# Attention scores from rounded halves in two passes a head, their loads on GpSimd, a shorter dt projection, and reordered stage ends

## The chip, the cores and the metric

The kernel runs on one core of a Trainium2 chip. Its engines are TensorE (PE: matrix products; PEld: its weight loads), VectorE (DVE), ScalarE (ACT), GpSimd (POOL) and SyncE (SP, which issues the transfers here), and 16 DMA engines. The metric is the device time of one execution in microseconds (us); lower is better.

## The reference

One layer of a hybrid encoder over two sequences (256 and 1024 rows, together T = 1280 columns in the kernel, where activations are kept transposed, features on the partitions). All in float32.

```
xn = rms_norm(x, g_mix)
q, k, v, gu, gv, z, xbc, dt_raw, gates = split(xn @ w_in)
# A: attention in a band of 128, 8 heads of 64 on 2 key heads
qn, kn = rms_norm(q, q_g) / 8, rms_norm(k, k_g)
scores = qn @ kn.T + bias            # a block of 128 queries sees 3 blocks of keys
out_A  = softmax_with_sink(scores) @ v
# B: out_B = gelu(gu) * (w_s @ layer_norm(gelu(gv)) + b_s)     per chunk of 128
# C: xbc = silu(conv(xbc)); dt = softplus(dt_raw + dt_bias)    2 directions x 16 heads
#    y = ssd_forward + ssd_backward + d * x                    chunks of 128
#    out_C = rms_norm(y * silu(z))
h = x + (sig(gA)*out_A@P_A + sig(gB)*out_B@P_B + sig(gC)*out_C@P_C) @ w_out
y = h + relu(rms_norm(h) @ w1)**2 @ w2
```

## The kernel before, in words

Every dense product is made of three passes in the rounded format f32r (`three_products`, L144): a weight tile and the activations are each split into a rounded high half and a remainder, and hi x hi, lo x hi and hi x lo are summed in PSUM. The 1280 columns go in three groups of 512, 512 and 256 (`GROUPS`); a tile of 128 output features takes 8 steps of 128 input features, so 24 passes a group. ScalarE makes the high half of a weight tile (L176), VectorE the remainder (L181).

Four stages follow one another, each ended by a barrier of all engines:

- `project` (0 to 418 us): the norm of x, then 26 of the tiles of the input projection; between the first ones, the norms of q and k, `dt_products` (behind tile 7) with `turn_dt`, the convolution.
- `attention_and_gmlp` (419 to 721): ten chunks of 128 queries in steps of some 26 us. The rest of the projection's tiles, the late ones (`LateTiles`), is spread over these steps: TensorE does some passes of a late tile (`late.product`) between two pairs of heads in `scores` and `values`. A late group's accumulator is read out by VectorE or ScalarE (`read_out`, L827 and L835).
- `state_space` (722 to 1159): ten chunks forwards, ten backwards (`LAST` is the last), with late tiles between. `finish_y` completes a chunk's y, `add_squares` and `sum_squares` its norm, `normalise` scales it. At the end y of the other branches is loaded and split ahead of the next stage (`ahead`).
- `merge` (1160 to the end): the up products, the output product and the feed-forward layer.

Each engine runs its instructions in the order in which they are written for it; engines wait for one another with semaphores (`wait_ge`, `then_inc`). All DMAs are issued by SyncE, in the order of its own list, and a wait in it holds up what stands behind.

Three places matter here. In `scores`, queries and keys of one key head lie on 64 partitions and those of the other on the other 64, in plain f32; a pair of heads is one product on each half:

```
for g in range(2):
    rows_of = slice(g * HD, (g + 1) * HD)
    pe.matmul(ps_s[:, g, 0:W], q[rows_of, s, j, :], k[rows_of, s, :],
              start=True, stop=True).then_inc(s_full, 1)
between(2 * j)
between(2 * j + 1)
```

`q` and `k` have two buffers (`s`), so a chunk's load can run two chunks ahead. `dt_products` are 8 x 3 passes a column group with 32 output columns (`dtw_hi`, `dtw_lo`), scaled afterwards by the root of x's norm. In `state_space` the wait for a chunk's loads (`loaded`) covers xbc, the factors and both rows of grown.

Of the kernel before, what the change touches and what calls it, by code (L numbers as in the profile page):

```python
# [62 lines left out]
def shape_constants():  # L63
# [25 lines left out]
    return {"masks": masks.astype(f), "onehot": onehot.astype(f), "edge": edge.astype(f)}  # L89
# [25 lines left out]
def build_layer(nc, a, scratch):  # L115

    with ExitStack() as ctx:
# [3 lines left out]
        with ExitStack() as inner:  # L121
            xn = [inner.enter_context(nc.sbuf_tensor(n, [P, KD, T], F32R)) for n in ("xn_hi", "xn_lo")]
            late = LateTiles(ctx, nc, lasting, ws, scratch, xn)
            ab = Split(lasting, "yab", xn)
            with nc.sbuf_tensor("late_result", [P, 2, T], F32) as late.result:
                with nc.sbuf_tensor("bias_sb", [P, HEADS, 3 * P], F32) as bias, nc.sbuf_tensor("root_sb", [P, T], F32) as root:
                    with stage_semaphores(nc) as sem:
                        project(nc, a, scratch, consts, ws, xn, bias, root, late, sem)
                    with stage_semaphores(nc) as sem:
                        attention_and_gmlp(nc, a, scratch, consts, bias, root, late, sem)  # L130
                with stage_semaphores(nc) as sem:
                    state_space(nc, a, scratch, consts, late, ab, sem)
            with stage_semaphores(nc) as sem:
                merge(nc, a, scratch, consts, ws, xn, ab, sem)
# [98 lines left out]
def project(nc, a, scratch, consts, ws, xn, bias, root, late, sem):  # L233
# [4 lines left out]
    with ExitStack() as ctx:  # L238
# [6 lines left out]
        qk_slot = (0, 1, 7)  # L245
        dtw = sb("dtw", [P, KD, 32])
        dtw_hi = sb("dtw_hi", [P, KD, 32], F32R)
        dtw_lo = sb("dtw_lo", [P, KD, 32], F32R)
# [9 lines left out]
        dt_T = sb("dt_T", [32, T])  # L258
# [25 lines left out]
        qk_ready = sem("qk_ready")  # L284
# [3 lines left out]
        stored = [sem(f"stored{s}") for s in range(3)]  # L288
# [8 lines left out]
        dtw_split = sem("dtw_split")  # L297
# [10 lines left out]
        qk_T, uv_T, xbc_T = (scratch[n] for n in ("qk_T", "uv_T", "xbc_T"))  # L308
        END = ((0, 511), (511, 1023), (1023, T))

        def free_at(slot, f):

            return f * 8 - (16 if slot == 0 else 24)

        with nc.Block() as block:
            @block.sync
            def _(sp):
                sp.dma_start(norm_g[:], a["norm_g"]).then_inc(gain_in, 16)
                ws.load(sp, 0, 0)
                for i, (g, lo, hi) in enumerate(PIECES):  # L320
                    t0, n = GROUPS[g]
                    sp.dma_start(x_T[:, lo:hi, t0:t0 + n], a["x_T"][:, lo:hi, t0:t0 + n]).then_inc(x_in[i], 16)
                    if i == 4:
                        ws.load(sp, 1, 1)
                sp.dma_start(masks[:], a["masks"]).then_inc(masks_in, 16)
# [3 lines left out]
                for dst, name in ((qk_g, "qk_g"), (conv_wb, "conv_wb"), (dtw, "w_dt")):  # L329
# [58 lines left out]
                for s, count in enumerate((2 + (N_EARLY - N_QKV) // 2, 3 + (N_EARLY - N_QKV) // 2, 1)):  # L388
                    sp.wait_ge(stored[s], 16 * count)
                sp.wait_ge(root_stored, 16)  # L390
# [7 lines left out]
            def _(pe):  # L398
                def dense(slot, tile):
# [3 lines left out]
                    for g, (t0, n) in enumerate(GROUPS):  # L403
                        if not (known and tile < 2):
# [41 lines left out]
                def dt_products():  # L446
                    pe.wait_ge(dtw_split, 2)
                    pe.wait_ge(scaled, 5)
                    for t0, n in GROUPS:
                        for k in range(KD):  # L450
                            mm = three_products(pe, aux[0:32, t0:t0 + n], dtw_hi[:, k], dtw_lo[:, k],
                                                xn_hi[:, k, t0:t0 + n], xn_lo[:, k, t0:t0 + n], k == 0, k == KD - 1)
                    mm.then_inc(dt_full, 1)

                def turn_v():
                    pe.wait_ge(dt_copied, 1)
# [5 lines left out]
                def turn_dt():  # L462
                    pe.wait_ge(v_ready, 1)
                    for c in range(NT):
                        mm = pe.transpose(aux[:, c * 32:(c + 1) * 32], dt_T[:, c * P:(c + 1) * P], masks[0:32, IDENT, 0:32])
                    mm.then_inc(dt_turned, 1)

                for f in range(F_XBC):
# [3 lines left out]
                    if f == 7:  # L472
# [18 lines left out]
            def _(act):  # L491
# [18 lines left out]

                def square(f):
# [15 lines left out]
                next_weights(0)  # L527
                norm.squares(act, 1)
# [5 lines left out]
                act.wait_ge(small_in, 16 * 5)  # L534
                act.activation(dtw_hi[:], dtw[:], ACT.Identity).then_inc(dtw_split, 1)
                for f in range(5):
                    square(f)
                    next_weights(f + 2)
                    root_of(f)

                def copy_rows(d):
                    act.wait_ge(rows_full, d + 1)
                    act.wait_ge(v_stored if d else stored[2], 16)
# [43 lines left out]
            def _(dve):  # L587
# [14 lines left out]
                def normalise(f):  # L602
# [3 lines left out]
                                             ALU.mult, ALU.mult).then_inc(qk_ready, 1)  # L606

# [8 lines left out]
                ws.low_half(dve, 1, 1)  # L616
                lower_x(2)
# [15 lines left out]
                dve.wait_ge(dtw_split, 1)  # L633
                dve.tensor_tensor(dtw_lo[:], dtw[:], dtw_hi[:].bitcast(F32), ALU.subtract).then_inc(dtw_split, 1)
# [45 lines left out]
                for f in range(2, F_XBC):  # L680
                    if f < 5:
                        out = x_T[:, qk_slot[f % 3]]
                        if f > 2:
                            dve.wait_ge(stored[f % 3], 16)
                    elif f == 5:
                        out = v_raw
                    else:
                        out = x_T[:, f % 2]
                        dve.wait_ge(stored[f % 2], free_at(f % 2, f))
# [5 lines left out]
                    if f == 7:  # L695
                        dve.wait_ge(dt_full, 1)
                        dve.tensor_tensor(dt_T[:], aux[0:32, 0:T], root[0:32], ALU.mult).then_inc(dt_copied, 1)
# [145 lines left out]
class RelativeBias:  # L843
# [39 lines left out]
    def store_rows(self, sp):  # L883
        sp.wait_ge(self.filled, 1)
        for lo in (0, P + T):
            sp.dma_start(self.scratch["qk_T"][4, :, lo:lo + P], self.zeros[:]).then_inc(self.pads_out, 16)
# [15 lines left out]
    def finish(self, sp):  # L902
        sp.wait_ge(self.shifted_in, 16)
        sp.wait_ge(self.pads_out, 64)


def attention_and_gmlp(nc, a, scratch, consts, bias, x_root, late, sem):
# [9 lines left out]
    with ExitStack() as ctx:  # L917
        def sb(name, shape):
# [1343 lines left out]
```

## Time and profile before

| | us |
|---|---|
| median of 3 runs | 2401.06 (2398.81 to 2401.78) |
| the profiled execution | 2400.81 |
| its span in the trace | 2399.0 |
| TensorE busy | 2335.7 (97%) |
| VectorE busy | 1157.5 (48%) |
| ScalarE busy | 841.8 (35%) |
| GpSimd busy | 0.2 (0%) |

Busy times overlap between engines. A matrix product's shown duration is longer than the distance to the next one, since products are pipelined; what a product costs is therefore read from the starts of successive rows. A plain-f32 product stands as two instructions in the rows. The mean granted clock is 0.991 of full speed.

### The profile page before, as it was taken

Reading aid. Unit: us, or ns where it says so; the run is one execution under the profiler, and the core shown is the slowest. Engines: PE = TensorE matmul, PEld = TensorE weight load, DVE = VectorE, ACT = ScalarE, POOL = GpSimd, SP = SyncE. Lnnn points to the kernel's source line nnn. Section 1 sums busy time; section 2 is a strip of 40 time slices with the busy share of each in tenths; the row PEclk is TensorE's granted clock in tenths of the full one; section 3 lists DMA queues with packets and bytes.
Section 4 is the critical chain, followed back from the end, with each engine's and each line's share of the span. In section 5 each row is a group of like instructions: output and inputs, shape, how many; then the busy total and the mean of one; then the engine's idle time right before and its main releaser. Section 6 shows DMA issues by size and latency. Waiting matters only on the chain.

```text
span 2399.0 us, 33028 instructions
## 1 busy us (share of the span) xinstructions
PE 2335.7 (97%) x12944; PEld 1953.3 (81%) x12944; DVE 1157.5 (48%) x1747; ACT 841.8 (35%) x1473; POOL 0.2 (0%) x4
## 2 busy tenths in 40 slices
PE   8999999899998999999799999999999999999999
PEld 6878888677776888887688888788888888888887
DVE  6223454566645666777677444433333333333333
ACT  7423322366655444666434132402021211112120
POOL 0000000000000000000000000000000000000000
PEclk9999999899999999999899999999999999999999
DMA  4223321333327777887563331111111111111112
GB/s 165 78 71 130 125 87 72 109 105 112 122 88 220 229 232 245 267 257 239 205 211 93 106 113 36 36 36 45 36 35 44 35 35 44 35 35 40 39 35 96
DMA packets 167020, 260.29 MB, mean 108 GB/s; under 512 B 11635, under 2 KB 119027, under 8 KB 164252
## 3 DMA queue, kind: packets, MB, share of 16 engines
q1 hardware_dynamic: 166940, 259.19, 33.3%
q8 instruction: 54, 0.88, 0.1%
q14 instruction: 26, 0.21, 0.0%
HBM read 191.54 MB, written 69.71 MB: 109 GB/s over the span
## 4 chain that ended last, share of the span: by engine, by line
PE 50%; DVE 1%; ACT 0%; DMA 0%; issue 0%; DVEq 0%
PE acc L146 16%; PE acc L147 16%; PE acc L148 16%; DVE xn_lo L1805 1%; DVE xn_lo L1803 0%; DMA merged<-s_y_T 0%; ACT xn_hi L1796 0%; PE acc L2079 0%; DVE gates L1924 0%; DVE h_T L2030 0%; ACT sums L2131 0%; ACT sums L2134 0%; ACT L2134 0%; ACT gates L2004 0%; DVE gates L2174 0%
## 5 line engine op out<-in xcount | busy, mean ns | idle before, releaser
L146 PE MATMUL acc<-xn_hi,w_hi 128*128 128x512 f32 (+1 forms) x1944 | 693.5, 357 | 22.1 <-DVE xn_lo L592 9.6
L147 PE MATMUL acc<-xn_hi,w_lo 128*128 128x512 f32 (+1 forms) x1944 | 690.9, 355 | 0.0
L148 PE MATMUL acc<-xn_lo,w_hi 128*128 128x512 f32 (+1 forms) x1944 | 689.9, 355 | 0.0
L146 PEld LDWEIGHTS acc<-xn_hi,w_hi 128*128 128x128 f32 x1944 | 369.2, 190 | 77.8 <-issue 13.9
L148 PEld LDWEIGHTS acc<-xn_lo,w_hi 128*128 128x128 f32 x1944 | 368.8, 190 | 51.7
L147 PEld LDWEIGHTS acc<-xn_hi,w_lo 128*128 128x128 f32 x1944 | 369.1, 190 | 51.2
L176 ACT ACTIVATE w_hi<-w_raw 128x1024 fp32r<-128x1024 f32 x146 | 153.6, 1052 | 555.9 <-PE acc L148 536.0
L146 PE MATMUL late_acc<-xn_hi,w_hi 128*128 128x512 f32 (+1 forms) x768 | 291.0, 379 | 8.2 <-DVE late_result L835 5.8
L148 PE MATMUL late_acc<-xn_lo,w_hi 128*128 128x512 f32 (+1 forms) x768 | 274.4, 357 | 0.0
L147 PE MATMUL late_acc<-xn_hi,w_lo 128*128 128x512 f32 (+1 forms) x768 | 273.8, 356 | 0.0
L147 PE MATMUL acc<-u_hi,w_lo 128*128 128x512 f32 (+1 forms) x768 | 273.6, 356 | 0.0
L146 PE MATMUL acc<-u_hi,w_hi 128*128 128x512 f32 (+1 forms) x768 | 273.6, 356 | 0.0
L148 PE MATMUL acc<-u_lo,w_hi 128*128 128x512 f32 (+1 forms) x768 | 273.6, 356 | 0.0
L2186 DVE TENSOR_TENSOR h_T<-h_T,acc 128x512 f32<-128x512 f32 (+1 forms) x192 | 114.8, 598 | 264.8 <-PE acc L148 264.8
L181 DVE TENSOR_TENSOR w_lo<-w_raw,w_hi 128x1024 fp32r<-128x1024 f32 x146 | 178.7, 1224 | 119.0 <-ACT w_hi L176 117.9
L146 PEld LDWEIGHTS late_acc<-xn_hi,w_hi 128*128 128x128 f32 x768 | 146.9, 191 | 52.5 <-issue 26.2
L147 PEld LDWEIGHTS late_acc<-xn_hi,w_lo 128*128 128x128 f32 x768 | 147.1, 192 | 21.3 <-issue 2.6
L148 PEld LDWEIGHTS late_acc<-xn_lo,w_hi 128*128 128x128 f32 x768 | 146.6, 191 | 20.9
L2144 ACT ACTIVATE u_hi<-gates 128x512 fp32r<-128x512 f32 (+1 forms) x96 | 53.9, 562 | 311.6 <-DVE gates L2174 311.6
L146 PEld LDWEIGHTS acc<-u_hi,w_hi 128*128 128x128 f32 x768 | 144.1, 188 | 23.5
L148 PEld LDWEIGHTS acc<-u_lo,w_hi 128*128 128x128 f32 x768 | 144.1, 188 | 23.5
L147 PEld LDWEIGHTS acc<-u_hi,w_lo 128*128 128x128 f32 x768 | 144.1, 188 | 23.5
(213 smaller groups left out, 2163.2 us busy)
## 6 DMA issues: line engine op xcount, KB each, us to landing
w_raw<-in_w_tiles SPq DMA_DIRECT2D x146, 512.0 KB, 3.7
s_late_T<-late_result SPq DMA_DIRECT2D x32, 640.0 KB, 6.5
c_w<-s_ac SPq DMA_DIRECT2D x20, 1024.0 KB, 4.7
c_grown<-s_grown SPq DMA_DIRECT2D x40, 256.0 KB, 5.6
gates<-s_late_T SPq DMA_DIRECT2D x16, 512.0 KB, 4.5
c_xbc<-s_xbc_T SPq DMA_DIRECT2D x10, 768.0 KB, 4.8
s_xbc_T<-x_T_sb SPq DMA_DIRECT2D x11, 640.0 KB, 3.0
gates<-s_late_T SPq DMA_DIRECT2D x24, 256.0 KB, 2.7
```

Of the source, the lines that this page charges most:

```text
L146: pe.matmul(out, w_hi, x_hi, start=first, stop=False)
L147: pe.matmul(out, w_lo, x_hi, start=False, stop=False)
L148: return pe.matmul(out, w_hi, x_lo, start=False, stop=last)
L176: act.activation(self.hi[:, s], self.raw[:, s], ACT.Identity).then_inc(self.hi_done, 1)
L181: dve.tensor_tensor(self.lo[:, s], self.raw[:, s], self.hi[:, s].bitcast(F32), ALU.subtract).then_inc(self.split_done, 1)
L1805: dve.scalar_tensor_tensor(low, src, self.gain[:, k:k + 1], high, ALU.mult, ALU.subtract).then_inc(self.low, 1)
L2144: act.activation(self.u_hi[:, i, t0:t0 + n], self.relu[:, u % 2, 0:n], ACT.Square).then_inc(self.high, 1)
L2186: dve.tensor_tensor(hh, hh, self.acc2[:, g, 0:n], ALU.add).then_inc(self.added, 1)
```

## The change

- The scores. After their norm, q and k are rounded by ScalarE (`qk_hi`), and VectorE subtracts (`qk_lo`); both are stored. For the scores a head's q has its high half on partitions 0 to 63 and its remainder on 64 to 127, and k's high half stands twice. A head then is one f32r pass of 128 rows (both halves of q with k's high half) and one of 64 rows (q's high half with k's remainder).
- Their loads. GpSimd issues them, into one buffer instead of two: for chunk c it waits until chunk c-1's scores are done.
- dt. `dt_products` move from behind tile 7 to behind tile 0, use raw x and weights times the norm's gain in plain f32, and put the eight steps of 128 features on four groups of 32 output columns, two steps to each. `turn_dt` sums the four groups while it transposes (`fold`).
- Start of attention: VectorE reads the first late result ahead of its next weight remainder; the passes of late tile 1, group 0 stand between the pairs of the first scores.
- State space: xbc has a semaphore of its own, which TensorE waits for; at the start the sums are loaded ahead of grown. At the end, the `ahead` loads are issued a step earlier, the last late group stands ahead of `sum_squares`, and VectorE's last `normalise` of the chunk before comes behind `finish_y`.
- Some buffers are shared or made per stage.

```diff
                 for f in range(5):
                     ws.load(sp, f % 2, f + 6)
-                    sp.wait_ge(qk_ready, f + 1)
-                    slot = f % 3
-                    sp.dma_start(qk_T[f, :, P:P + T], x_T[:, qk_slot[slot]]).then_inc(stored[slot], 16)
+                    for kind, (half, done) in enumerate(((qk_hi, qk_high), (qk_lo, qk_low))):
+                        sp.wait_ge(done, f + 1)
+                        if f == 4:
+                            sp.dma_start(scratch["k_halves"][kind, :, P:P + T], half[:].bitcast(F32)).then_inc(qk_stored, 16)
+                            continue
+                        for g in range(2):
+                            sp.dma_start(scratch["q_halves"][4 * g + f, kind], half[g * HD:(g + 1) * HD].bitcast(F32)).then_inc(qk_stored, 16)
...
                 def dt_products():
-                    pe.wait_ge(dtw_split, 2)
+
+                    pe.wait_ge(dtw_ready, 1)
+                    for t0, n in GROUPS:
+                        for half in range(2):
+                            for i in range(4):
+                                k = 4 * half + i
+                                mm = pe.matmul(aux[32 * i:32 * i + 32, t0:t0 + n], dtw[:, k], x_T[:, k, t0:t0 + n],
+                                               start=half == 0, stop=half == 1)
+                        mm.then_inc(dt_full, 1)
...
                     for c in range(NT):
-                        mm = pe.transpose(aux[:, c * 32:(c + 1) * 32], dt_T[:, c * P:(c + 1) * P], masks[0:32, IDENT, 0:32])
+                        mm = pe.matmul(aux[:, c * 32:(c + 1) * 32], dt_T[:, c * P:(c + 1) * P], fold[:], start=True, stop=True)
...
                 ws.low_half(dve, 1, 1)
+                dve.wait_ge(dtw_in, 16)
+                dve.tensor_tensor(dtw[:], dtw[:], norm_g[:, 0].unsqueeze(2).to_broadcast([P, KD, 32]), ALU.mult).then_inc(dtw_ready, 1)
                 lower_x(2)
...
-        q = sb("q_sb", [P, 2, 4, P])
-        k = sb("k_sb", [P, 2, W])
+        q = sb("q_halves_sb", [P, HEADS, P], F32R)
+        k_hi = sb("k_hi_twice", [P, 2, W], F32R)
+        k_lo = sb("k_lo_sb", [HD, 2, W], F32R)
...
+            @block.gpsimd
+            def _(pool):
+                def load_qk(s, chunk):
+
+                    t0 = chunk * P
+                    if not first(chunk):
+                        pool.wait_ge(s_full, chunk * 8)
+                    if not first(chunk, 2):
+                        pool.wait_ge(m_ready, chunk - 1)
+                    pool.dma_start(q[:], scratch["q_halves"][:, :, :, bass.ds(t0, P)].rearrange("h i d t -> (i d) h t").bitcast(F32R)).then_inc(qk_in[s], 16)
...
-                    for j in range(HEADS // 2):
-                        if not (first(chunk) and j == 0):
-                            pe.wait_ge(s_read, chunk * 8 + 2 * j)
...
-                        between(2 * j)
-                        between(2 * j + 1)
+                    for i, h in enumerate(ORDER):
+                        if not (first(chunk) and i < 2):
+                            pe.wait_ge(s_read, chunk * 8 + (i - 1))
+                        pe.matmul(ps_s[:, i % 2, 0:W], q[:, h], k_hi[:, h // 4], start=True, stop=False)
+                        pe.matmul(ps_s[:, i % 2, 0:W], q[0:HD, h], k_lo[:, h // 4], start=False, stop=True).then_inc(s_full, 1)
+                        if i % 2:
+                            between(i - 1)
+                            between(i)
...
-                scores(0, 0, 48)
+                scores(0, 0, 80, lambda h: late.product(pe, 1, 1, 0, [h]))
...
-                for g in range(NG):
+                for g in range(1, NG):
                     late.product(pe, 1, 1, g)
...
-                late.low_half(dve, 1, 1)
                 for g in range(2):
                     late.read_out_with(dve, 0, 0, g, x_root)
+                late.low_half(dve, 1, 1)
...
+                    if isinstance(n, int) and n == LAST - 1:
+                        sp.wait_ge(y_full, LAST)
+                        for k in range(KD):
+                            sp.dma_start(ahead[k], scratch["y_T"][k, :, 0:512]).then_inc(ahead_in[k // 4], 16)
...
-                    pe.wait_ge(loaded[s], came)
+                    pe.wait_ge(xbc_in[s], came)
...
                         late.product(pe, s, n + BEFORE, 1)
+                        late.product(pe, s, n + BEFORE, 2)
                         sum_squares(n)
-                        late.product(pe, s, n + BEFORE, 2)
...
-                for k in range(2):
-                    ab.remainder(dve, 0, k, ahead[k])
                 finish_y(1, LAST, 1, 16 * NT // 2)
-                for k in range(2, 4):
+                normalise(0, LAST - 1)
+                for k in range(4):
                     ab.remainder(dve, 0, k, ahead[k])
                 add_squares(LAST)
```

How the rows stand then. First TensorE at the start of attention, from the last pass of late tile 0: before, the eight plain-f32 products of the first scores, then the first product with ln_b's rows and late tile 1.

```order
L148 MATMUL late_acc<-xn_lo,w_hi 128x256
L1033 MATMUL ps_scores<-k_sb,q_sb 128x384 x8
L1105 MATMUL ps_gmlp<-w_sT,ln_b_rows 128x128 x4
L146 MATMUL late_acc<-xn_hi,w_hi 128x512
L147 MATMUL late_acc<-xn_hi,w_lo 128x512
```

And with the change:

```order
L148 MATMUL late_acc<-xn_lo,w_hi 128x256
L1073 MATMUL ps_scores<-k_hi_twice,q_halves_sb 128x384
L1074 MATMUL ps_scores<-k_lo_sb,q_halves_sb 128x384
L1073 MATMUL ps_scores<-k_hi_twice,q_halves_sb 128x384
L1074 MATMUL ps_scores<-k_lo_sb,q_halves_sb 128x384
L146 MATMUL late_acc<-xn_hi,w_hi 128x512
L147 MATMUL late_acc<-xn_hi,w_lo 128x512
L148 MATMUL late_acc<-xn_lo,w_hi 128x512
```

L1073 is a pass of 128 rows, L1074 one of 64; they alternate, and six late passes (L146 to L148, twice) stand behind each pair of heads, in the first chunk too.

Next, VectorE at the end of the state-space stage. The names: c_y is y, c_w, c_x_end and c_kept hold the rows loaded ahead, xn_lo their remainders. Before:

```order
L1691 TENSOR_TENSOR c_y<-s_bank_a,c_grown 128x1024
L1655 TENSOR_TENSOR c_y<-c_y,c_y_root 128x1024
L1803 TENSOR_TENSOR xn_lo<-c_w,xn_hi 128x512 x2
L1628 TENSOR_TENSOR c_y<-c_y,s_bank_b 128x1024
L1632 TENSOR_TENSOR c_y<-c_y,c_other 128x1024
L1635 TENSOR_TENSOR c_y<-c_y,c_z 128x1024
L1803 TENSOR_TENSOR xn_lo<-c_w,xn_hi 128x512 x2
L1648 TENSOR_TENSOR c_y_sq<-c_y_sq 128x2x256
```

With the change:

```order
L1746 TENSOR_TENSOR c_y<-s_bank_a,c_grown 128x1024
L1683 TENSOR_TENSOR c_y<-c_y,s_bank_b 128x1024
L1687 TENSOR_TENSOR c_y<-c_y,c_other 128x1024
L1690 TENSOR_TENSOR c_y<-c_y,c_z 128x1024
L1710 TENSOR_TENSOR c_y<-c_y,c_y_root 128x1024
L1857 TENSOR_TENSOR xn_lo<-c_w,xn_hi 128x512 x4
L1703 TENSOR_TENSOR c_y_sq<-c_y_sq 128x2x256
```

The three steps that finish the last chunk's y (L1683 to L1690) stand directly behind the product with grown; the scaling of the chunk before (L1710, L1655 before) and all four remainders of c_w come behind them.

Last, GpSimd's list in the loop over the chunks; before, it had no row in this stage.

```order
L1052 ISA
L1052 DMA q_halves_sb<-s_q_halves 128x8x128
L1054 DMA k_hi_twice<-s_k_halves 64x2x384 x2
L1054 ISA
L1054 DMA k_lo_sb<-s_k_halves 64x2x384
```

These are the loads of one chunk, behind the wait for the last scores of the chunk before (the row in front of q's load).

## Rows read from the trace of the kernel before

**Rows 1.** The page, part 1: busy us (share), instructions.

```profile
PE 2335.7 (97%) x12944; PEld 1953.3 (81%) x12944; DVE 1157.5 (48%) x1747; ACT 841.8 (35%) x1473; POOL 0.2 (0%) x4
```

**Rows 2.** The waits of TensorE: total us, times, longest.

```profile
PE s_bank_d L1530 <- DVE c_y_sq L1650: 11.5, 1, 11.5
...
PE late_acc L146 <- DVE late_result L835: 5.8, 2, 4.1
PE s_bank_a L1473 <- DMA c_grown<-s_grown: 5.6, 1, 5.6
```

**Rows 3.** Timeline of TensorE, dt: start, us, instruction, [idle before].

```profile
135.64 0.39 PE L146 MATMUL aux<-xn_hi,dtw_hi 128*32 128x512 f32 x1
...
149.30 0.28 PE L148 MATMUL aux<-xn_lo,dtw_hi 128*32 128x256 f32 x1
149.42 0.40 PE L146 MATMUL acc<-xn_hi,w_hi 128*128 128x512 f32 x1
```

**Rows 4.** Timeline of TensorE, a plain-f32 product between passes.

```profile
31.45 0.40 PE L148 MATMUL aux<-xn_lo,w_hi 128*128 128x512 f32 x1
31.68 1.02 PE L219 MATMUL late_acc<-root_sb,masks_sb 128*128 128x512 f32 x2
...
32.77 0.40 PE L147 MATMUL aux<-xn_hi,w_lo 128*128 128x512 f32 x1
```

**Rows 5.** Timeline of TensorE, products with v.

```profile
478.24 0.88 PE L1053 MATMUL ps_out<-probs_T,v_sb 128*64 128x128 f32 x12
479.05 0.39 PE L146 MATMUL late_acc<-xn_hi,w_hi 128*128 128x256 f32 x1
```

**Rows 6.** Timeline of TensorE, the transposes of dt.

```profile
179.31 0.80 PE L465 MATMUL aux<-masks_sb,dt_T 32*128 32x32 f32 x10
```

**Rows 7.** Timeline of VectorE, end of the state-space stage.

```profile
1129.93 1.22 DVE L1691 TENSOR_TENSOR c_y<-s_bank_a,c_grown 128x1024 f32<-128x1024 f32 x1
...
1145.77 1.29 DVE L1803 TENSOR_TENSOR xn_lo<-c_w,xn_hi 128x512 fp32r<-128x512 f32 x2
...
1147.70 0.42 DVE L1650 TENSOR_TENSOR c_y_sq<-c_y_sq 128x256 f32<-128x256 f32 x1
...
1151.67 1.23 DVE L1655 TENSOR_TENSOR c_y<-c_y,c_y_root 128x1024 f32<-128x1024 f32 x1 [1.14 <-ACT c_y_root L1569]
```

**Rows 8.** Timeline of TensorE, two pairs of heads in a steady chunk.

```profile
482.87 0.40 PE L148 MATMUL late_acc<-xn_lo,w_hi 128*128 128x512 f32 x1
483.20 0.92 PE L1033 MATMUL ps_scores<-k_sb,q_sb 64*128 64x384 f32 x4
484.05 0.50 PE L146 MATMUL late_acc<-xn_hi,w_hi 128*128 128x512 f32 x1
...
485.62 0.92 PE L1033 MATMUL ps_scores<-k_sb,q_sb 64*128 64x384 f32 x4
```

**Rows 9.** Timeline of TensorE, start of attention to the third chunk's scores, then of ScalarE.

```profile
427.89 1.16 PE L1033 MATMUL ps_scores<-k_sb,q_sb 64*128 64x384 f32 x4
...
435.01 1.65 PE L1033 MATMUL ps_scores<-k_sb,q_sb 64*128 64x384 f32 x4 [1.11 <-DVE scores_sb L1125]
...
451.34 0.39 PE L146 MATMUL late_acc<-xn_hi,w_hi 128*128 128x256 f32 x1 [1.70 <-DVE late_result L835]
...
454.40 0.92 PE L1033 MATMUL ps_scores<-k_sb,q_sb 64*128 64x384 f32 x4
...
480.76 0.92 PE L1033 MATMUL ps_scores<-k_sb,q_sb 64*128 64x384 f32 x4
...
443.40 0.62 ACT L1226 ACTIVATE scores_sb<-scores_sb,softmax_stat 128x384 f32<-128x384 f32 x1 [21.55 <-DVE softmax_stat L1141]
...
448.31 1.04 ACT L176 ACTIVATE w_hi<-w_raw 128x1024 fp32r<-128x1024 f32 x1
```

**Rows 10.** DMA issues: line, count, KB each, us to landing.

```profile
q_sb<-s_qk_T SPq DMA_DIRECT2D x10, 256.0 KB, 4.6
```

**Rows 11.** Timeline of ScalarE, then of TensorE, start of state space.

```profile
733.55 4.77 ACT L1553 ACTIVATE c_w<-c_w,c_factors 128x128 f32<-128x128 f32 x16
...
747.40 1.97 PE L1517 MATMUL s_bank_b<-c_w,c_x_dt 128*64 128x128 f32 x32 [2.18 <-DVE c_state L1695]
```

**Rows 12.** Timeline of SyncE, end of the state-space stage.

```profile
1154.38 0.40 SPq L1400 DMA_DIRECT2D s_y_T<-c_y  x1
1159.73 0.39 SPq L1854 DMA_DIRECT2D merged<-s_y_T  x1
```

More of the change, by code:

```diff
@@ L283, in project @@
         rooted = sem("qk_rooted")
-        qk_ready = sem("qk_ready")
+        qk_ready, qk_high, qk_low, qk_stored = (sem("qk_" + n) for n in ("ready", "high", "low", "stored"))
         curved = sem("uv_curved")
@@ L287, in project @@
         end_step, end_done = sem("end_step"), sem("end_done")
-        stored = [sem(f"stored{s}") for s in range(3)]
+        stored = [sem(f"stored{s}") for s in range(2)]
         root_stored = sem("root_stored")
@@ L403, in dense @@
                     for g, (t0, n) in enumerate(GROUPS):
+                        if known and tile == 1:
+                            pe.wait_ge(dt_copied, g + 1)
                         if not (known and tile < 2):
@@ L471, in _ @@
                         sum_squares(f - 2)
[L472 removed]
+                    if f == 0:
                         dt_products()
@@ L1001, in step @@
                 def step(s, chunk, loads, gated_tile):
-                    if loads:
-                        load_qk(s, chunk + 2)
                     late.load(sp, s, chunk + 4)
@@ L1021, in _ @@
                     sp.wait_ge(y_stored[s], 16 * NT // 2)
+            @block.gpsimd
[7 more added lines that the diff above has]
+                    pool.dma_start(q[:], scratch["q_halves"][:, :, :, bass.ds(t0, P)].rearrange("h i d t -> (i d) h t").bitcast(F32R)).then_inc(qk_in[s], 16)
+                    for i, to in enumerate((k_hi[0:HD], k_hi[HD:P], k_lo[:])):
+                        pool.dma_start(to, scratch["k_halves"][i // 2, :, bass.ds(t0, W)].rearrange("(g d) t -> d g t", g=2)
+                                       .bitcast(F32R)).then_inc(qk_in[s], 16)
+                    pool.dma_start(edge[:, s], a["edge"][bass.ds(chunk, 1)].rearrange("o p e -> p (o e)")).then_inc(qk_in[s], 16)
+                load_qk(0, 0)
+                load_qk(1, 1)
+                with pool.Fori(1, NT // 2) as pair:
+                    for s in range(2):
+                        load_qk(s, pair * 2 + s)
             @block.tensor
@@ L1321, in state_space @@
         ahead_in = [sem(f"s_ahead_in{i}") for i in range(2)]
+        xbc_in = [sem(f"s_xbc_in{s}") for s in range(2)]
         tok_stored, tok_in = ([sem(f"s_{n}{s}") for s in range(2)] for n in ("tok_stored", "tok_in"))
@@ L1430, in step @@
                     store(s, n, c, d)
+                load_xbc(0, 0, 0)
+                load_factors(0, 0, 0)
+                load_sums(0, 0, 0)
+                load_grown(0, 0, 0)
                 sp.dma_start(d_col[:], a["d_col"]).then_inc(col_in, 16)
-                for i in range(2):
-                    load(i, i, 0)
-                    load_sums(i, i, 0)
+                load(1, 1, 0)
+                load_sums(1, 1, 0)
                 with sp.Fori(0, NT // 2 - 1) as pair:
@@ L1450, in _ @@
                         step(s, n, LAST - n, 1, LAST - 2 - n, 1)
-                step(0, LAST - 1, *chunk_of(LAST - 1), None, None)
-                sp.wait_ge(y_full, LAST)
-                for k in range(KD):
-                    sp.dma_start(ahead[k], scratch["y_T"][k, :, 0:512]).then_inc(ahead_in[k // 4], 16)
-                step(1, LAST, *chunk_of(LAST), None, None)
+                for n in (LAST - 1, LAST):
+                    step(n % 2, n, *chunk_of(n), None, None)
                 late.all_stored(sp, BEFORE + 2 * NT)
@@ L1695, in step @@
                         dve.tensor_tensor(state[:], kept[:], bank_b[:], ALU.add).then_inc(state_ready, 1)
-                    if normal:
+                    if normal and not is_last(n):
                         normalise(1 - s, n - 1)
```

155 lines of the change are left out of this document (81 added, 74 removed).

## The prediction

> **What bounds the kernel now.** The page's first part comes first: TensorE is busy for 2335.7 us of 2399.0 and VectorE for 48% [rows 1]. Time moves only with TensorE's own passes, or with the few places where it stands still. The list of TensorE's waits gives those places [rows 2]: 11.5 us at the end of the state-space stage, 5.8 at the start of attention, 5.6 at the start of the state-space stage. Each part of the change meets either a run of passes or one of these waits. The sum is made against the profiled execution, 2400.8 us (span 2399.0), 0.25 us under the median of 2401.06. About 0.2%, 4.8 us, is what a measurement of this kernel can tell from no change.
>
> **dt projection.** Now 72 passes run from 135.64 to 149.42, 13.8 us [rows 3]. They go, and 24 plain-f32 products come behind tile 0: eight for each of the three column groups of 512, 512 and 256. One such product of 512 columns takes 32.77 - 31.68 less the pass of 0.23 (31.68 - 31.45) that stands in between, 0.86 us [rows 4]. One after another, the 24 would take 8 x 2.5 x 0.86 = 17.2; with the four 32-column groups side by side, 4.3. For side by side speak the products with v, which use two 64-column groups: six products of 128 columns would take 6 x 0.86/4 = 1.28 one after another, and are done in 479.05 - 478.24 = 0.81 [rows 5]. No row has four groups; I take 4.3 and 0.6 for entering and leaving, 4.9. Turning dt is ten 32-row transposes now, 0.8 [rows 6], and becomes ten plain-f32 products with 128 rows of weights; at some 0.1 for each of their two instructions, 2.1: +1.3. VectorE gets a multiplication of 128 x 256 ahead of the last part of x's remainder, for which TensorE waits at that point of the program; a row of that size is 0.42 [rows 7]. Sum: -13.8 + 4.9 + 1.3 + 0.4 = **-7.2**, at worst +5 (serial).
>
> **Halves of q and k.** Five roundings on ScalarE, five subtractions on VectorE, 18 stores in place of 5. A subtraction of 1024 columns is some 1.22 [rows 7], so 1.5 for 1280. They stand once a tile of some 17 us of TensorE's passes, on engines that are idle for half the time [rows 1]: 0. If nothing hid them, VectorE's five would show with +7.5.
>
> **Scores.** Now two heads are two plain-f32 products on the two halves of the rows at once. A pair of heads with its six late passes repeats every 485.62 - 483.20 = 2.42 us [rows 8]. The six passes are 6 x 0.23 = 1.37, so the pair costs 1.05. Its stream alone is 0.86 x 384/512 = 0.64. The other 0.41 is the price of entering and leaving the 64-row layout, 0.2 each; half of the entry can be read directly: the scores start 483.20 - 482.87 = 0.33 behind the last late pass, where late passes start 0.23 apart, and 484.05 - 483.20 = 0.85 is left for the stream and the exit. Plain f32 alone has no such price, since the 0.86 of rows 4 is four bare passes of some 0.215.
>
> The new pair is four f32r passes of 0.23 x 384/512 = 0.17, in the order 128 rows, 64, 128, 64, and then the late passes, which are 128 again. The stream, 0.69, is no shorter than now, and there are four changes of layout where there were two: 0.69 + 0.8 = 1.49, +0.44 a pair. The first pair of a chunk comes from the v products, which have a layout of their own, so it has five changes instead of two: +0.64. A chunk costs 3 x 0.44 + 0.64 = 1.96 more, and nine chunks **+17.6** (the first chunk is in the next term). This is the largest term, and it hangs on the 0.2. Bounds: with no price at all a pair is 0.69 instead of 1.05 and a chunk gains 1.24, -11.2 over nine; with 0.3 for each change it is +33. I take 0.2, since rows 8 have the same 64 rows.
>
> The Trainium skill, "TensorEngine Tiling (Array Packing)", section Tiling Modes, Key Properties, says that a change of the tiling mode, and not of the tile alone, drains TensorE. The 0.41 us around a pair agrees with it. By that rule the new order drains four times a pair, which is the sum above; were a switch free, the stage would gain 11.
>
> **Loads by GpSimd.** q and both halves of k now land in one buffer instead of two, so a chunk's load can be issued only after the last score of the chunk before. A step is 480.76 - 454.40 = 26.4 us [rows 9]; the new scores with the passes between them take 3 x (1.49 + 1.37) + 1.49 = 10.1 of it. That leaves 16.3 us for 512 KB of q and 576 KB of k. SyncE's 256 KB of q land in a median of 4.6 [rows 10]; four times the bytes, if they took four times as long, would be 18. No row shows a load issued by GpSimd. I take 8 to 14, hidden: 0. From 16.3 on, each us shows almost in full, eight times.
>
> **Start of attention.** VectorE reads the first late result before it lowers a weight, which saves about 2 of the 4.1 us that TensorE waits [rows 2]. But the first scores wait for GpSimd's first loads; I take 428, about where they start now (427.89, rows 9). One late group of 5.5 us (24 passes) is moved in between them, away from behind them. From the last score (435.01 + 1.65 = 436.66) to the late group at 451.34 there are 14.7 us of VectorE's bias and maxima, ScalarE's exponents from 443.40 and weight at 448.31, VectorE's weight and read-out [rows 9]. Beside these, TensorE will have some 7 us of work instead of 13. The last score ends at 428 + 3 x 2.86 + 1.5, and 2 more for the half clock that is seen here (1.65 for four instructions that take 0.92 later, rows 8 and 9): 440. With 14.7: 454.8. The late group behind it, 3.06 now (454.40 - 451.34), takes about twice that after 7 us of idling: 461, and the second chunk's scores, still at half clock, lose another 1 to 2. Against 454.40: **+8**, from 0 (early loads, no clock lost) to +14 (loads 5 us late).
>
> **Start of the state-space stage.** TensorE waits 5.6 us for c_grown, the last of its loads [rows 2], and would now wait for xbc alone. But behind it ScalarE's decays run from 733.55, and the products that need them start at 747.40 [rows 11]; they hang on the sums, which move ahead of grown by two issues only. **-1.5**, from 0 to -2.2.
>
> **End of the state-space stage.** The merge's first rows of y are loaded after the last chunk's products instead of after the store of the chunk before, some 13 us earlier. VectorE, which waited for ScalarE's rounding of them, goes straight on at 1129.93 + 1.2 = 1131.1 [rows 7]: three steps of 1.2 that finish y, one of 1.2 that scales the chunk before, four remainders of 0.62 (1.29 for two less overlap), two squares (1.1). The squares end at 1139.6, now at 1148.1. Behind them, the scaled y follows after 4.8 (1151.67 + 1.23 - 1148.1, rows 7), its store at 1154.38, and the merge's first load 5.35 after the store [rows 12]. With the same steps y is ready at 1144.4, and the merge starts at 1149.8 instead of 1159.73: **-10**, from -7 to -11. TensorE's 11.5 us of waiting becomes a wait for the new stage.
>
> **Sum.** 2400.8 - 7.2 + 17.6 + 8 - 1.5 - 10 = 2407.7. The moved buffers cost nothing: no instruction waits for them in place of another.
>
> **The rivals.**
> (a) The 64-row f32r passes pay nothing for a change. For it: the 72 passes of 32 columns, f32r in a narrow layout, pay nothing (24 x (0.23 + 0.23 + 0.12) = 13.9 against 13.8, the 0.12 from 149.42 - 149.30, rows 3). Against it: rows 8, which have the rows halved, not the columns. Then 2400.8 - 7.2 - 11.2 + 6 - 1.5 - 10 = 2377, faster. The change as a whole breaks even at 0.155 a change of layout: 9 x (17 x 0.155 - 1.44) = 10.7, what the other terms give.
> (b) GpSimd's loads land more than 16.3 us after the last score. For it: 1088 KB in short rows, into one buffer. Against it: 4.6 us for a quarter of the bytes, and a queue of their own. With 20 us, 8 x 3.7 = 30, more with a lost clock: 2438 to 2457.
> (c) The four 32-column groups run one after another: +12.9, 2421.
> (d) The stage ends do not give their 11.5 back, since another load of the new stage lands last: 2419.
>
> **Chances.** The forecast as summed 0.58, its own range 2399 to 2417; (a) 0.18; (b) 0.12; (c) 0.06; (d) 0.06. The range reaches down to (a) and up past (c): 2374 to 2424; it leaves out (b). Faster, under 2396, 0.20: (a) and a little of the forecast; same, up to 2405.6, 0.23: its lower part; slower 0.57.
>
> **What would show it.** A pair with its passes every 2.86 us in the steady chunks (2.06 if (a) holds); dt's products done within 5 us behind tile 0 (17 in (c)); no wait for q's load ahead of the scores, or one (b); some 7 us of idling ahead of the second chunk's late group; the merge's first load some 10 us earlier against the stage's start. The prediction is wrong above all if a change between two f32r layouts has another price than between f32r and plain f32.

## The result and the profile after

The changed kernel takes 2413.34 us in the median of five runs (2409.16 to 2414.68), the kernel before 2400.14 in its five: a ratio of 1.005, 95% interval 1.0035 to 1.0065. That is slower by 13 us; the forecast was 2408, with a range of 2374 to 2424. The profiled execution took 2410.82, with a span of 2408.4, 9.4 more than before's.

Where the 9.4 us lie is read from one event at each stage's border, the difference between before and after being taken from one border to the next. All times are starts in us, except that the first row is an end.

| border | before | after | after less before, since the border above |
|---|---|---|---|
| project's last pass done, TensorE idle | 418.36 | 411.21 | -7.15 |
| second chunk's scores | 454.40 | 455.60 | +8.35 |
| last products with v | 714.08 | 733.01 | +17.73 |
| last chunk's y products (state space) | 1129.02 | 1149.50 | +1.55 |
| merge's first load | 1159.73 | 1169.27 | -10.94 |
| end of the span | 2399.0 | 2408.4 | -0.14 |

The list of TensorE's waits of the changed kernel (total us, times, longest one), beside [rows 2]:

```profile
PE acc L146 <- PEq L113: 8.6, 1, 8.6
PE late_acc L146 <- DVE late_result_a L865: 8.3, 2, 6.3
PE ps_scores L1073 <- DMA edge_sb<-in_edge: 6.2, 1, 6.2
PE s_bank_b L1560 <- DVE c_x_end L1729: 6.1, 1, 6.1
```

Before, the list also had:

```profile
PE acc L146 <- PEq L112: 6.5, 1, 6.5
```

The 11.5 us for s_bank_d are gone; the wait at the next stage's start has grown from 6.5 to 8.6 (PEq is TensorE's sequencer behind the barrier). New are 6.2 us for GpSimd's first loads and 6.3 ahead of the second chunk's late group (1.7 there before). The 5.6 for c_grown have become 6.1 for c_x_end. What VectorE's steps around c_x_end wait for stands in its timeline:

```profile
754.25 0.42 DVE L1720 COPY c_b_tok<-s_bank_c 128x256 f32<-128x256 f32 x1 [12.13 <-DMA c_d_col<-in_d_col]
754.59 0.42 DVE L1721 TENSOR_TENSOR c_cb<-s_bank_c,masks_sb 128x256 f32<-128x256 f32 x1
754.92 1.22 DVE L1729 TENSOR_TENSOR c_x_end<-c_x_tok,c_factors 128x1024 f32<-128x1024 f32 x1
...
762.08 1.23 DVE L1741 TENSOR_TENSOR c_w<-c_w,c_cb 128x1024 f32<-128x1024 f32 x1 [3.66 <-ACT c_w L1610]
```

c_d_col is the skip column. The change issues it last of the stage's first loads, where before it came first; the description of the change leaves this out. VectorE's first step waits for it, but a few steps later VectorE waits another 3.66 us for ScalarE's decays, so it is the decays that end last here.

The timeline of TensorE for dt, beside [rows 3] and [rows 6]:

```profile
27.02 4.50 PE L461 MATMUL aux<-x_T_sb,dtw 128*32 128x512 f32 x48
...
31.45 0.50 PE L146 MATMUL aux<-xn_hi,w_hi 128*128 128x512 f32 x1
...
170.79 2.31 PE L477 MATMUL aux<-fold_sb,dt_T 128*128 128x32 f32 x20
```

The 24 products (48 instructions) take 31.45 - 27.02 = 4.43 us; the turning takes 2.31.

The timeline of TensorE in a steady chunk, beside [rows 8]:

```profile
539.69 0.88 PE L1094 MATMUL ps_out<-probs_T,v_sb 128*64 128x128 f32 x12
540.50 0.44 PE L1073 MATMUL ps_scores<-k_hi_twice,q_halves_sb 128*128 128x384 f32 x1
540.87 0.43 PE L1074 MATMUL ps_scores<-k_lo_sb,q_halves_sb 64*128 64x384 f32 x1
541.24 0.44 PE L1073 MATMUL ps_scores<-k_hi_twice,q_halves_sb 128*128 128x384 f32 x1
541.61 0.44 PE L1074 MATMUL ps_scores<-k_lo_sb,q_halves_sb 64*128 64x384 f32 x1
541.98 0.50 PE L146 MATMUL late_acc<-xn_hi,w_hi 128*128 128x512 f32 x1
...
543.47 0.34 PE L1073 MATMUL ps_scores<-k_hi_twice,q_halves_sb 128*128 128x384 f32 x1
543.74 0.44 PE L1074 MATMUL ps_scores<-k_lo_sb,q_halves_sb 64*128 64x384 f32 x1
...
546.36 0.34 PE L1073 MATMUL ps_scores<-k_hi_twice,q_halves_sb 128*128 128x384 f32 x1
```

The starts of the four passes lie 0.37 apart, where a pass of 384 columns streams for 0.17. Entered from the late passes (543.47), the first pass, still in their layout, takes only 0.27 until the 64-row pass starts. A pair with its six late passes repeats every 2.89 us (546.36 - 543.47; 2.87 for later ones), before 2.42. The step from chunk to chunk is 28.33 us (540.50 to 568.83), before 26.35.

DMA issues of GpSimd (count, KB each, median us to landing) and the first two rows of its timeline for one chunk:

```profile
q_halves_sb<-s_q_halves POOLq DMA_DIRECT2D x10, 512.0 KB, 7.3
...
edge_sb<-in_edge POOLq DMA_DIRECT2D x10, 2.0 KB, 9.4
```

```profile
466.46 0.89 POOL L1052 DMA_DIRECT2D q_halves_sb<-s_q_halves  x1 [25.88 <-PE ps_scores L1074]
...
469.10 0.65 POOL L1056 DMA_DIRECT2D edge_sb<-in_edge  x1
```

The last of a chunk's loads lands about 469.1 + 9.4 = 478.5, 12 us after the first issue; the scores that need them start at 483.83.

The timeline of SyncE at the end of the state-space stage, beside [rows 12]:

```profile
1164.49 0.38 SPq L1451 DMA_DIRECT2D s_y_T<-c_y  x1
1169.27 0.40 SPq L1908 DMA_DIRECT2D merged<-s_y_T  x1
```

The last y is stored 1164.49 - 1149.50 = 15.0 us after the last chunk's products, 25.4 before (1154.38 - 1129.02).

### The profile page after: what moved, and what is told of

Read it like the earlier page. It is cut to its first block, busy times and chain, and to the rows that moved or that the text cites. A ratio compares the mean times of both kernels' runs of the same rounds, so it can differ in the third digit from the quotient of the medians.

```text
span 2408.4 us, 33121 instructions
## 1 busy us (share of the span) xinstructions
PE 2347.7 (97%) x12930; PEld 1964.3 (82%) x12930; DVE 1169.6 (49%) x1752; ACT 849.6 (35%) x1480; POOL 33.3 (1%) x54
## 4 chain that ended last, share of the span: by engine, by line
PE 49%; DVE 1%; ACT 0%; DMA 0%; issue 0%; DVEq 0%
PE acc L146 16%; PE acc L147 16%; PE acc L148 16%; DVE xn_lo L1859 1%; DVE xn_lo L1857 0%; DMA merged<-s_y_T 0%; ACT xn_hi L1850 0%; PE acc L2133 0%; DVE gates L1978 0%; DVE h_T L2084 0%; ACT sums L2185 0%; ACT sums L2188 0%; ACT L2188 0%; ACT gates L2058 0%; DVE gates L2228 0%
## 5 line engine op out<-in xcount | busy, mean ns | idle before, releaser
L146 PE MATMUL acc<-xn_hi,w_hi 128*128 128x512 f32 (+1 forms) x1944 | 693.9, 357 | 24.3 <-DVE xn_lo L615 9.6
L148 PE MATMUL acc<-xn_lo,w_hi 128*128 128x512 f32 (+1 forms) x1944 | 690.0, 355 | 0.0
L146 PEld LDWEIGHTS acc<-xn_hi,w_hi 128*128 128x128 f32 x1944 | 369.3, 190 | 80.2 <-issue 16.2
L148 PEld LDWEIGHTS acc<-xn_lo,w_hi 128*128 128x128 f32 x1944 | 368.8, 190 | 52.0
L146 PE MATMUL late_acc<-xn_hi,w_hi 128*128 128x512 f32 (+1 forms) x768 | 292.0, 380 | 9.7 <-DVE late_result_a L865 8.3
L148 PE MATMUL late_acc<-xn_lo,w_hi 128*128 128x512 f32 (+1 forms) x768 | 274.9, 358 | 0.0
L146 PE MATMUL acc<-u_hi,w_hi 128*128 128x512 f32 (+1 forms) x768 | 273.6, 356 | 0.0
L148 PE MATMUL acc<-u_lo,w_hi 128*128 128x512 f32 (+1 forms) x768 | 273.6, 356 | 0.0
L146 PEld LDWEIGHTS late_acc<-xn_hi,w_hi 128*128 128x128 f32 x768 | 147.0, 191 | 41.8 <-issue 14.5
L148 PEld LDWEIGHTS late_acc<-xn_lo,w_hi 128*128 128x128 f32 x768 | 146.7, 191 | 21.3
L146 PEld LDWEIGHTS acc<-u_hi,w_hi 128*128 128x128 f32 x768 | 144.1, 188 | 23.5
L148 PEld LDWEIGHTS acc<-u_lo,w_hi 128*128 128x128 f32 x768 | 144.1, 188 | 23.5
```

Source lines behind the costliest of these rows:

```text
L146: pe.matmul(out, w_hi, x_hi, start=first, stop=False)
L148: return pe.matmul(out, w_hi, x_lo, start=False, stop=last)
```

## The experiments

Unless another base is named, each is the changed kernel with the one edit shown, and its time stands against the 2413.3 of the change. Ratios are to the kernel before, which took 2399.4 to 2401.1 in the median beside them, so a difference of a microsecond between medians says nothing; where spans of profiled executions differ from medians, both are given.

**The order within a pair.**

```diff
-pe.matmul(ps_s[:, i % 2, 0:W], q[:, h], k_hi[:, h // 4], start=True, stop=False)
-pe.matmul(ps_s[:, i % 2, 0:W], q[0:HD, h], k_lo[:, h // 4], start=False, stop=True)
+high = (q[:, h], k_hi[:, h // 4])
+low = (q[0:HD, h], k_lo[:, h // 4])
+one, two = (low, high) if i % 2 else (high, low)
+pe.matmul(ps_s[:, i % 2, 0:W], *one, start=True, stop=False)
+pe.matmul(ps_s[:, i % 2, 0:W], *two, start=False, stop=True)
```

> The change with the second head of a pair taking its 64-row pass first, so that a pair reads 128, 64, 64, 128 rows: the same eight passes a pair of pairs, two changes of layout fewer a pair. If a change of layout costs 0.2 us, a pair with its six late passes repeats every 2.46 us instead of 2.87, a chunk gains 1.6 and the whole 16: about 2397. If the 64-row pass itself is slow (0.37 instead of 0.17), or a second pass into the same accumulator, the pair stays at 2.87 and the time at 2413.

2394.25 us (ratio 0.9974, 0.9964 to 0.9983), 19 less than the change and already faster than before. The timeline of TensorE, one pair and the start of the next:

```profile
538.60 0.34 PE L1076 MATMUL ps_scores<-k_hi_twice,q_halves_sb 128*128 128x384 f32 x1
538.87 0.44 PE L1077 MATMUL ps_scores<-k_lo_sb,q_halves_sb 64*128 64x384 f32 x1
539.15 0.33 PE L1076 MATMUL ps_scores<-k_lo_sb,q_halves_sb 64*128 64x384 f32 x1
539.42 0.44 PE L1077 MATMUL ps_scores<-k_hi_twice,q_halves_sb 128*128 128x384 f32 x1
...
541.09 0.33 PE L1076 MATMUL ps_scores<-k_hi_twice,q_halves_sb 128*128 128x384 f32 x1
```

The same four passes, and the pair repeats every 2.49 us instead of 2.87 to 2.89: 0.38 to 0.40 for two changes of layout fewer, 0.19 to 0.2 each. From one pass's start to the next it is 0.27 or 0.28 where the layout changes at one end of the pass, and was 0.37 where it changed at both. The 64-row pass as such isn't slow, and neither is a second pass into an accumulator.

**Both passes on 128 rows.** Rows 64 to 127 of k's remainder are zeros that SyncE loads once, so the second pass sums the same products.

```diff
-k_lo = sb("k_lo_sb", [HD, 2, W], F32R)
+k_lo = sb("k_lo_sb", [P, 2, W], F32R)
...
-pe.matmul(ps_s[:, i % 2, 0:W], q[0:HD, h], k_lo[:, h // 4], start=False, stop=True)
+pe.matmul(ps_s[:, i % 2, 0:W], q[:, h], k_lo[:, h // 4], start=False, stop=True)
```

> The change with both passes of a head on 128 rows: k's remainder stands on 128 partitions, the lower 64 filled with zeros once, and q's both halves are the weights of the second pass too. No change of layout is left inside the scores. If the change of layout (or the 64-row pass) costs the time, the pair goes to 0.69 + 1.37 = 2.06 us, a chunk gains 3.2, ten chunks 32: about 2381. If the second pass into the same accumulator costs it, nothing moves: 2413.

2382.62 us (ratio 0.9929, 0.9912 to 0.9945), 31 less than the change (28 between the profiled spans). The timeline of TensorE for the first pair of a chunk:

```profile
528.34 0.44 PE L1077 MATMUL ps_scores<-k_hi_twice,q_halves_sb 128*128 128x384 f32 x1
528.62 0.34 PE L1078 MATMUL ps_scores<-k_lo_sb,q_halves_sb 128*128 128x384 f32 x1
528.79 0.35 PE L1077 MATMUL ps_scores<-k_hi_twice,q_halves_sb 128*128 128x384 f32 x1
528.98 0.34 PE L1078 MATMUL ps_scores<-k_lo_sb,q_halves_sb 128*128 128x384 f32 x1
529.15 0.40 PE L146 MATMUL late_acc<-xn_hi,w_hi 128*128 128x512 f32 x1
```

Inside the pair the passes follow at 0.17 to 0.19, and only the first, coming from the v products, pays 0.28. Two heads cost less (0.70 in a later pair) than the plain-f32 pair of before (1.05). The step is 26.0 to 26.1 us and not the 25.1 that follows from 28.3 less 3.2: TensorE now waits 0.8 us a chunk for the probabilities (0.34 with the change) and 0.3 for the turned v, so most of what is missing goes into waits for ScalarE and VectorE behind the scores.

**First scores in one piece.**

```diff
-scores(0, 0, 80, lambda h: late.product(pe, 1, 1, 0, [h]))
+scores(0, 0, 80)
...
-for g in range(1, NG):
+for g in range(NG):
     late.product(pe, 1, 1, g)
```

> The change with the first scores in one piece again, late tile 1's group 0 behind them. If the pause of 6.4 us ahead of the second chunk's late group comes from the passes that were moved from behind the last score to ahead of it, the pause falls under 2 us and the second chunk's scores start 4 to 5 us earlier: about 2409. If the half clock eats it, or the pause comes from the loads, 0 to 2 us: 2411 to 2413.

2404.60 us (ratio 1.0018, 1.0008 to 1.0028). The wait ahead of the late group is gone from the list of waits, and the second chunk's scores start at 451.25, 40.3 after project's end against 44.4. The time fell by 8.7 in the medians and by 5.2 between the profiled spans; the trace accounts for 4.1 of it.

**Order of the state-space stage's first loads.** As before; the skip column is `d_col`, `load` is xbc, factors and grown.

```diff
-load_xbc(0, 0, 0)
-load_factors(0, 0, 0)
-load_sums(0, 0, 0)
-load_grown(0, 0, 0)
-sp.dma_start(d_col[:], a["d_col"]).then_inc(col_in, 16)
+sp.dma_start(d_col[:], a["d_col"]).then_inc(col_in, 16)
+load(0, 0, 0)
+load_sums(0, 0, 0)
```

> The change with the first loads of the state-space stage in the order of before (the skip column first, xbc, factors, grown, then the sums), TensorE still waiting for xbc alone. If sums ahead of grown and the column behind both make ScalarE's decays and VectorE's first step late, the decays start 1.5 to 3 us earlier against the stage's first transfer and the time falls by as much: about 2411. If the loads take what they take in any order, 0: 2413.

2409.18 us (ratio 1.0035, 1.0022 to 1.0047). The timeline of ScalarE, of the change and of this run:

```profile
754.04 4.78 ACT L1608 ACTIVATE c_w<-c_w,c_factors 128x128 f32<-128x128 f32 x16 [5.94 <-DMA c_grown<-s_grown]
```

```profile
754.53 4.79 ACT L1606 ACTIVATE c_w<-c_w,c_factors 128x128 f32<-128x128 f32 x16 [3.25 <-DMA c_w<-s_ac]
```

xbc is issued at 740.94 in the change and at 743.25 here, so the decays start 13.1 and 11.3 us after it (before: 733.55 - 722.37 = 11.2, the issue being at 722.37). In the change ScalarE is released by grown, here by the sums. The last chunk's y products come 406.9 us after xbc's issue, 1.7 less than in the change; as xbc itself stands behind the skip column here and is issued 0.4 later, the stage gains 1.3. The medians fell by 4.2 and the profiled spans by 0.8, since attention's start took 1.9 longer in this execution.

**Grown with a semaphore of its own.** ScalarE's decays wait for factors and sums alone (the counts of `loaded` fall from 48 to 16 a chunk); the skip column is issued ahead of grown.

```diff
-    .to_broadcast([SHD, 8, P])).then_inc(loaded[s], 16)
+    .to_broadcast([SHD, 8, P])).then_inc(grown_in[s], 16)
...
+dve.wait_ge(grown_in[s], came[1])
 dve.tensor_tensor(y[:, s], bank_a[:], grown[:, s].rearrange("p j t -> p (j t)"), ALU.mult)
```

> The change with a semaphore of their own for both rows of grown, which VectorE waits for only where it multiplies by them; ScalarE's decays then wait for the factors and the sums alone, and the skip column is loaded ahead of grown. If the decays are late because they wait for grown, which now stands behind the sums, they start at 9 to 11 us after the stage's first transfer instead of 13.1 and the time falls by 2 to 4: about 2410. If all transfers of the stage's start share one stream and the sums land last anyway, they start at 11.3 as in the order of before: 2411 to 2412.

2409.60 us (ratio 1.0037, 1.0023 to 1.0051). The decays start at 752.70, 10.7 us after xbc's issue at 741.98, released by the sums. The last chunk's y products come 407.8 us after that issue (change 408.6, before 406.7, old load order 406.9), so of the 2.4 us by which the decays are earlier, 0.8 are left at the end of the stage. The timelines of TensorE, of the change and of this run, show where the rest goes:

```profile
767.89 1.97 PE L1572 MATMUL s_bank_b<-c_w,c_x_dt 128*64 128x128 f32 x32 [1.42 <-DVE c_state L1750]
769.79 1.10 PE L1528 MATMUL s_bank_a<-masks_sb,c_xbc 128*128 128x128 f32 x8
770.72 0.38 PE L1534 MATMUL s_bank_c<-masks_sb,c_xbc 128*128 128x128 f32 x2
```

```profile
766.55 2.85 PE L1572 MATMUL s_bank_b<-c_w,c_x_dt 128*64 128x128 f32 x32 [2.17 <-DVE c_state L1751]
769.33 1.83 PE L1528 MATMUL s_bank_a<-masks_sb,c_xbc 128*128 128x128 f32 x8
770.99 0.38 PE L1534 MATMUL s_bank_c<-masks_sb,c_xbc 128*128 128x128 f32 x2
```

The products with c_w do start 2.4 us earlier after xbc's issue (24.57 against 26.95). But they take 2.78 instead of 1.90, and the products behind them 1.66 instead of 0.93: the granted clock is 0.67 and 0.58 of full speed in these two stretches, so most of each runs at the lower of TensorE's two levels (1.2 and 2.4 GHz), after waits of 1.55 and 2.17 us; in the change it was 1.00 in both. That is 1.6 of the 2.4.

**End of the state-space stage as before.**

```diff
+for k in range(2):
+    ab.remainder(dve, 0, k, ahead[k])
 finish_y(1, LAST, 1, 16 * NT // 2)
-normalise(0, LAST - 1)
-for k in range(4):
+for k in range(2, 4):
     ab.remainder(dve, 0, k, ahead[k])
```

Here `normalise(0, LAST - 1)` stands in the last step again, with the loads ahead behind step LAST-1 and the last late group behind `sum_squares`.

> The change with the end of the state-space stage as before (the loads for the merge after the store of the last chunk but one, VectorE's and TensorE's old order). If that part gives the 10 us that the traces show, the merge's first load comes 30.7 us after the last chunk's products start, as before, instead of 19.8, and the time rises by 10 to 11: about 2424. If something later gives it back, 0 to 3: 2413 to 2416.

2423.59 us (ratio 1.0099, 1.0082 to 1.0116), 10.3 more than the change. The merge's first load starts at 1181.30, 30.5 us behind the last y products (1150.82); in the change 1169.27 - 1149.50 = 19.8.

**dt's products one after another.**

```diff
-pe.matmul(aux[32 * i:32 * i + 32, t0:t0 + n], dtw[:, k], ..., start=half == 0, stop=half == 1)
+pe.matmul(aux[0:32, t0:t0 + n], dtw[:, k], ..., start=k == 0, stop=k == KD - 1)
```

> The change with dt's eight products of a column group all on the first group of 32 output columns, so that none stands beside another; the fold then takes 32 rows. If the four column groups run at once, the products take 17 us instead of 4.4 and the time rises by 12.7: about 2426. If they do not overlap, or TensorE's time there is hidden, 0: 2413.

2423.65 us (ratio 1.0101, 1.0084 to 1.0118); by the trace:

```profile
26.89 17.37 PE L461 MATMUL aux<-x_T_sb,dtw 128*32 128x512 f32 x48
...
44.20 0.50 PE L146 MATMUL aux<-xn_hi,w_hi 128*128 128x512 f32 x1
```

17.31 us instead of 4.43: four column groups do run at once. The profiled span grew by 12.5, the medians by 10.3.

**Together.** Both passes on 128 rows, first scores in one piece, first loads in the old order.

> The change with the three edits together: k's remainder on 128 rows, first scores in one piece, first state-space loads in the order of before. If their gains are separate: 2382.6 less 4 to 8 (first scores) less 2 to 4 (loads), about 2373. If a common cause (the softmax chain behind TensorE) bounds attention's start, 2377 to 2380.

2376.92 us (ratio 0.9905, 0.9888 to 0.9921). That is 4 above the 2373 for separate gains and just below the range for a common cause. By the profiled spans the three gain 32.6 together and 33.8 alone, nearly the same; by the medians it is 36.4 against 43.6, so whether they are fully separate stays open.

**The first chunk's loads by SyncE**, on top of that, at the head of its list.

```diff
+sp.dma_start(q[:].bitcast(F32), scratch["q_halves"][:, :, :, 0:P].rearrange("h i d t -> (i d) h t")).then_inc(first_in, 16)
+for i, to in enumerate((k_hi[0:HD], k_hi[HD:P], k_lo[0:HD])):
+    sp.dma_start(to.bitcast(F32), scratch["k_halves"][i // 2, :, 0:W].rearrange("(g d) t -> d g t", g=2)).then_inc(first_in, 16)
...
-load_qk(0, 0)
```

> As the run before it, and the first chunk's q and k issued by SyncE at the head of its list instead of by GpSimd. If GpSimd's first loads, whose last lands about 8 us after its issue and 11 after the stage's first, make the first scores late, these start 2 to 4 us earlier, and the time is 2 to 4 lower. If another engine or the bytes set the start, 0.

2374.42 us (ratio 0.9894, 0.9877 to 0.9910). Timelines of TensorE, of the run before it and of this one:

```profile
422.95 0.66 PE L1077 MATMUL ps_scores<-k_hi_twice,q_halves_sb 128*128 128x384 f32 x1 [6.46 <-DMA edge_sb<-in_edge]
```

```profile
419.48 0.69 PE L1080 MATMUL ps_scores<-k_hi_twice,q_halves_sb 128*128 128x384 f32 x1 [3.30 <-DMA k_lo_sb<-s_k_halves]
```

The first scores start 3.5 us earlier, the second chunk's 4.1 (443.56 against 447.70); 2.5 are left in the medians, 3.9 in the profiled spans.

**All of it, and grown's own semaphore.**

> The fastest version so far (k's remainder on 128 rows, first scores in one piece, first loads by SyncE) with grown's own semaphore and sums, skip column, grown in this order. Against its 2374.4: 0 to 2 lower if the decays start earlier than 10.9 us after the first transfer, 0 if the sums land last anyway.

2373.24 us (ratio 0.9886, 0.9869 to 0.9902), the fastest version, 27 us under the kernel before. Against 2374.42 the last edit cannot be told from no change.

**The changed kernel once more.**

> The changed kernel once more, unedited, for a second profile: its profiled execution was 2.5 us below its median. If the start of attention varies with the landing of GpSimd's first loads, the second chunk's scores start 0 to 3 us later than 455.6 here and the rest of the profile is the same; if the difference lies elsewhere, another stage differs.

2412.09 us (2411.38 to 2413.61 in four runs); profiled execution 2411.57, span 2408.7. From project's end to the third chunk's scores it takes 73.1 us, against 72.6 in the first profile; runs whose attention is the same take 73.9 (grown's own semaphore) to 74.5 (old load order). So the start of attention varies by up to 2 us from run to run, and both profiles of the change lie at its lower end. That can account for up to 1.9 of the 2.5 us between the first profile and its median, though no profile at the median shows it.

## Why the prediction was right, point by point

- **Scores**, +17.6 forecast, +17.7 measured. A steady pair costs 2.87 less the 1.37 of its late passes, 1.50 (1.49 forecast), a change of layout 0.19 to 0.2 (0.2), and a step 28.33 - 26.35 = 1.98 more than before (1.96). The Trainium skill's rule ("TensorEngine Tiling (Array Packing)", Tiling Modes, Key Properties: a change of mode drains, a change of tile doesn't) agrees: two 64-row passes in a row are 0.28 apart, 0.37 where the layout changes on both sides. Rival (a), that f32r passes pay nothing, would have had a pair every 2.06 and is refuted by 2.87. The order within a pair and the 128-row version show the cause by taking away two changes and all of them.
- **dt**, -7.2 forecast, -7.15 measured. The products took 4.4 (4.9) and the turning 2.3 (2.1), which makes -7.8; the first passes on the third column group start at 23.69 instead of 22.98, 0.7 later (0.4 for VectorE's multiplication). That leaves nothing for the halves of q and k, which were forecast to be hidden. Rival (c) is refuted: the four groups took 4.4 us and, one after another, 17.3.
- **Loads by GpSimd**, hidden: true for the steady chunks, 12 us of 16.3. Rival (b) is refuted there. The Trainium skill, "DMA: Bandwidth & Descriptors", section "Anatomy of one DMA — SWDGE (gpsimd) path", has a fit of 2.0 us plus bytes over 436e3 per us, which gives an estimate of 3.2 for q; here a median of 7.3 was measured, with four other loads issued behind it, and the measurement stands.
- **Start of attention**, +8 forecast, +8.35 measured, but two errors cancel, so that the size agrees is luck. GpSimd's first loads were taken to be in time for scores at 428; less the 7.15 won before, that is 420.9, and the scores started at 423.98. On the other side the late group that pauses was taken to run at half clock to its end; the granted clock was 0.50 only up to 454.4, so the group took 455.60 - 451.23 = 4.37, not 6, and the scores behind it lost nothing. The two causes have prices of their own: the reordered late group 4.1 (first scores in one piece), the first loads 3.5 (by SyncE).
- **Start of the state-space stage**, -1.5 forecast, +1.55 measured: the step that failed. It counted on ScalarE's decays hanging on the sums alone. Their wait covers grown too, and grown was moved behind the sums, which are 1024 KB; its landing now releases them, 1.9 us later after xbc's issue than before. TensorE's earlier start on xbc only changed what it waits for next. The old load order takes 1.3 us of it back. And the move of the sums could not give much: they release the decays 10.7 us after xbc's issue where they stand ahead of grown, 11.3 where behind.
- **End of the state-space stage**, -10 forecast, -10.94 measured, and 10.3 in the run that takes the part back. Rival (d) is refuted. The last y is stored 10.4 us earlier against the last products, and the merge's first load follows the store after 4.8 us (5.35 forecast). TensorE's wait did not move into the next stage, as the prediction had it: of 11.5 us, 2.1 were added there (6.5 to 8.6).

So the sum came out 5.6 us below the median: 3.1 from the loads of the state-space stage less 0.9 from its end, 2.5 since the median lies that far above the profiled execution, and the remaining microsecond from small differences.

## What to carry to other kernels

Count the changes of TensorE's row layout in the written order, not the passes: 128, 64, 128, 64 rows cost as much for switching (0.8 us) as for streaming (0.69), and filling up the 64-row operand with zeros gave more back (31 us) than the whole change lost (13). When a load is moved ahead in a queue, look at every semaphore that the overtaken load feeds, and at what waits for them. A pause that is shortened at one place by moving work there must be paid with the cover that the work gave where it stood.

## What the runs showed that was not expected

- A 64-row pass between 128-row passes is dearer than a 128-row pass with half of its rows zero: 0.37 against 0.17 to 0.19 us for 384 columns.
- GpSimd's five issues of a chunk take 3.3 us of its time (469.10 + 0.65 - 466.46), and the last of them, 2 KB, lands only a median of 9.4 us after its issue, behind the 1 MB issued ahead of it.
- With the scores at 0.70 a pair, the attention step takes 26.0 to 26.1 us, not 25.1: TensorE waits 1.1 us of it for ScalarE and VectorE.
- Decays that start 2.4 us earlier left 0.8, since TensorE's granted clock stood at 0.58 to 0.67 in the products behind them.
